# A two-layer hybrid trunk on eight cores: the mixer runs its 31-tap convolution path first, x of two token groups of the next tile is staged in idle buffers, and the last step of v's norm may run on VectorE or GpSimd

## The reference

```python
x = x + 0.5 * rms_norm(swiglu(rms_norm(x, f1_pre), f1_wg, f1_wu, f1_wd), f1_post)     # 1024 -> 2816 -> 1024
z = rms_norm(x, m_pre) @ w_in                                                        # 1024 -> 2304
a_val, a_c, a_b, b_u, b_v, c_val, c_gate = split(z)      # 3 x 256, 2 x 512, 2 x 256 columns
y_a = a_b * conv3(a_c * a_val)
v   = layer_norm(gelu(b_v), per head of 128)
y_b = gelu(b_u) * (tril(W_s) @ v + bias)                 # mixes the tokens of a chunk of 128
y_c = silu(layer_norm(conv31(c_val * sigmoid(c_gate)) + c_cb))
x = x + rms_norm(concat(y_a, y_b, y_c) @ w_out, m_post)
x = x + 0.5 * rms_norm(swiglu(rms_norm(x, f2_pre), f2_wg, f2_wu, f2_wd), f2_post)
x = x + rms_norm(sigmoid(rms_norm(x, e_pre) @ e_wg) * (p[i] @ e_wp), e_post)
```

## Time and profile before

| | us |
|---|---|
| three runs | 2700.43, 3136.25, 2699.31 |
| median | 2700.43 |
| profiled execution | 2699.21 |
| its span, slowest core (core 5) | 2697.6 |
| spans of all cores | 2689.7 to 2697.6 |
| PE busy | 2581.1 (96%) |
| DVE busy | 1148.4 (43%) |
| ACT busy | 1070.5 (40%) |
| POOL busy | 558.5 (21%) |
| mean granted PE clock by core | 0.986 to 0.989 |

### The profile page before, as it was taken

The page is one execution under the profiler, slowest core; times in us unless marked ns, Lnnn a source line. Parts: engine busy times, 40 slices in busy tenths (PEclk is TensorE's granted clock), DMA queues, the critical chain, the costliest instruction groups (busy, mean ns, idle before and its releaser), DMA issues.

```text
span 2697.6 us, 52916 instructions; the slowest of 8 cores (2689.7 to 2697.6 us)
## 1 busy us (share of the span) xinstructions
PE 2581.1 (96%) x18576; PEld 1685.2 (62%) x18576; DVE 1148.4 (43%) x2748; ACT 1070.5 (40%) x2199; POOL 558.5 (21%) x880
## 2 busy tenths in 40 slices
PE   6999989999999998999969999999999999999996
PEld 3676556666567655666637665667665676656764
DVE  2222774216621476421642137632175215672227
ACT  3123474126512356312632135731264124671235
POOL 0052212004205211200410412210052132120014
PEclk9999999999999999999989999999999999999998
DMA  8354323334344532333564454233343444423341
GB/s 161 61 89 82 69 50 64 74 65 82 64 76 79 89 65 49 63 71 65 115 159 81 74 90 65 40 75 69 65 71 75 75 71 91 64 49 71 67 82 64
DMA packets 53442, 204.38 MB, mean 76 GB/s; under 512 B 10528, under 2 KB 22592, under 8 KB 38304
## 3 DMA queue, kind: packets, MB, share of 16 engines
q0 software_dynamic: 32608, 178.81, 37.7%
q1 hardware_dynamic: 20576, 22.18, 2.8%
HBM read 371.12 MB, written 9.63 MB: 141 GB/s over the span
## 4 chain that ended last, share of the span: by engine, by line
PE 91%; ACT 3%; issue 2%; DVE 2%; DMA 1%; POOL 1%; SPq 0%; DVEq 0%; ACTq 0%; POOLq 0%
PE PS L614 89%; PE PS L620 2%; ACT L490 1%; ACT SCR L645 1%; DVE XT L656 1%; DMA XT<-xT 1%; DMA RING<-W 0%; DMA yT<-SCR 0%; SPq L684 0%; ACT SQS L645 0%; ACT R L645 0%; DVE SCR L663 0%; POOL R L651 0%; ACT PS L645 0%; POOL XT L656 0%
## 5 line engine op out<-in xcount | busy, mean ns | idle before, releaser
L614 PE MATMUL PS<-R,RING 128*128 128x256 bf16 (+2 forms) x10560 | 1617.3, 311 | 36.0 <-ACT SCR L645 19.5
L614 PEld LDWEIGHTS PS<-R,RING 128*128 128x128 bf16 x10560 | 1032.8, 98 | 541.1 <-issue 62.1
L614 PE MATMUL PS<-HIDR,RING 128*128 128x256 bf16 (+2 forms) x4992 | 767.7, 311 | 2.7 <-ACT HIDR L645 1.1
L645 ACT ACTIVATE SCR<-PS 128x256 f32<-128x256 f32 (+3 forms) x818 | 374.8, 463 | 980.0 <-PE PS L614 947.7
L656 DVE TENSOR_TENSOR HIDR<-SCR,PS 128x512 bf16<-128x512 f32 (+2 forms) x552 | 282.1, 512 | 891.6 <-PE PS L614 881.1
L614 PEld LDWEIGHTS PS<-HIDR,RING 128*128 128x128 bf16 x4992 | 489.6, 98 | 259.0 <-issue 8.0
L684 POOL DMA_DIRECT2D RING<-W x192 | 106.3, 554 | 1615.3 <-PE PS L614 1583.9
L645 ACT ACTIVATE SQS<-PS 128x256 bf16<-128x256 f32 (+2 forms) x288 | 132.0, 458 | 428.3 <-PE PS L614 426.7
L656 POOL TENSOR_TENSOR XT<-XT,SCR 128x256 f32<-128x256 f32 (+2 forms) x210 | 194.2, 934 | 397.3 <-DVE SCR L663 358.1
L663 DVE SCALAR_TENSOR_TENSOR R<-XT,VECT,PS 128x256 bf16<-128x256 f32 (+2 forms) x376 | 188.9, 565 | 70.2 <-ACT PS L645 58.7
L490 ACT ACT_TABLE_LOAD x147 | 188.6, 1283 | 2.6
(11 more groups left out here) (91 smaller groups left out, 1034.3 us busy)
## 6 DMA issues: line engine op xcount, KB each, us to landing
RING<-W POOLq DMA_DIRECT2D x116, 1024.0 KB, 8.5
RING<-W POOLq DMA_DIRECT2D x64, 704.0 KB, 6.1
RING<-W POOLq DMA_DIRECT2D x8, 768.0 KB, 6.3
XT<-xT SPq DMA_DIRECT2D x8, 512.0 KB, 9.5
XT<-xT SPq DMA_DIRECT2D x16, 256.0 KB, 9.6
yT<-SCR SPq DMA_DIRECT2D x16, 256.0 KB, 3.2
yT<-SCR SPq DMA_DIRECT2D x32, 128.0 KB, 2.1
RING<-W POOLq DMA_DIRECT2D x4, 512.0 KB, 5.0
```

The costliest lines, as they stand in the source:

```text
L614: S.add("pe", lambda e: e.matmul(out.build(), lhsT.build(), rhs.build(), start=start, stop=stop), r=[lhsT, rhs], w=[out], dur=max(n, 64) / ...
L645: return e.activation(out=out.build(), in_=in_.build(), func=func, **k2)
```

## The change

It has three parts.

1. In the mixer, `inC` becomes the first slot. Its matmuls, the convolution and the layer norm of group C are recorded with the slot numbers of the first slot. The token mix of group B goes behind `inU`. The block of code for path C is moved as it was, word for word, except that the token mix no longer stands inside it.
2. x of the first two groups of the second tile is staged in idle parts of `R1` and `HIDR` (16 transfers in place of 8). Only the third group waits for its place in `XT`. Both staged groups are loaded into `XT` later, when ACT has done a Silu of slot 9 of the tile's first feed-forward block. Slots 4 to 10 of the tile now wait for all four transfers of the third group.
3. The last step of v's norm may run on POOL as well; the layout chooses for each one.

```diff
-            plan += [(("inA", 0), 3072), (("inA", 1), 3072), (("inV", 0), 4096), (("inU", 0), 4096),
-                     (("inC", 0), 4096), (("out", 0), 4096), (("out", 1), 4096)]
+            plan += [(("inC", 0), 4096), (("inA", 0), 3072), (("inA", 1), 3072), (("inV", 0), 4096), (("inU", 0), 4096),
+                     (("out", 0), 4096), (("out", 1), 4096)]
...
-    def TS(out, in0, s1, s2, op0, op1, n, prio, eng="dve", acq=(), tag="", after=()):
+    def TS(out, in0, s1, s2, op0, op1, n, prio, eng="dve", acq=(), tag="", after=(), alt=False):
...
+              alt=("pool", 0.2 + n * 0.0021) if alt else None)
...
-            w0 = subs[0][1]
-            stage = []
-            for c0, n, _, _, _ in TILES[ti - 1]:
-                a = 8 * c0 + 4 * n
...
+            prev = TILES[ti - 1]
+            idle = []
+            for c0, n, _, _, _ in prev:
+                idle.append([R1t, 8 * c0 + 4 * n, 8 * c0 + 8 * n, 1])
+                idle.append([HIDt, JC * c0 + 16 * n, JC * (c0 + n), 2])
+            for si in range(2):
+                w0, t0_ = subs[si][1], subs[si][2]
+                chunks = []
...
+                stage[si] = chunks
+                for k in range(KC):
+                    dst = fx(chunks[k])
+                    DMA("sp", dst, raw(xv[:, k, tok0 + t0_:tok0 + t0_ + w0]), [], [dst], "c_x", 128 * w0 * 4, (0, g0 - 20 + 10 * si), tag="xs", slack=10.0)
...
+        def reload(gate):
+            if ti:
+                for si in stage:
+                    xload(si, gate, (1, g0 + 6), 0.0)
+
+        for si in range(nsub):
+            if si not in stage:
+                xload(si, [xl[0][-1]] if ti == 0 and si else [], (0, g0 + 0.01 * si - 1), 4.0 if ti else 0.0)
...
-            for i in range(slot_n[0] + 3, slot_n[0] + 11):
-                gates[i] = xl[1][:2]
+            for i in range(slot_n[0] + 4, slot_n[0] + 11):
+                gates[i] = xl[2]
...
-                src = (lambda k, si=si: fx(stage[k])) if stage and si == 0 else (lambda k, si=si: Xs(si, k))
+                src = (lambda k, si=si: fx(stage[si][k])) if si in stage else (lambda k, si=si: Xs(si, k))
...
+            if l == 0 and f == 1:
+                reload([early[0]])
...
+            wC = wload(l, ("inC", 0))
             wA = [wload(l, ("inA", 0)), wload(l, ("inA", 1))]
-            wV, wU, wC = wload(l, ("inV", 0)), wload(l, ("inU", 0)), wload(l, ("inC", 0))
+            wV, wU = wload(l, ("inV", 0)), wload(l, ("inU", 0))
...
-                               ALU.subtract, ALU.mult, 128, (0, g))
+                               ALU.subtract, ALU.mult, 128, (0, g), alt=True)
...
-                gsp = wC.g + skew(si) + 0.3
+                gsp = wU.g + skew(si) + 0.3
```

135 lines of the change are left out of this document (67 added, 68 removed).

## The result

The changed kernel takes 2667.44 us, the median of its four runs, against 2700.43 shown before. The ratio is **0.9876**, 95% interval 0.9848 to 0.9905: 1.2% faster, within the 2% of no change. Executions in which one die ran at a lower clock throughout are left out of every comparison from here on, and a time is the median of the others. The profiled execution took 2664.45 us with a span of 2662.7; before it was 2699.21 and 2697.6. The forecast was 2664, with a range of 2642 to 2694.

A forecast was written before the change was run, and what follows sets the result against it. PE was taken to bound the kernel, busy 2581.1 of 2697.6 us. Terms -20.9 (change of tile), -19.7 (mixer ends) and +4 (mixer fronts) sum to -36.6 us: 2662.6 profiled, 2664 us as median; range 2642 to 2694.

The forecast's parts named there:

- v's last step: Mixer: moving 52 of 128 norm steps from DVE to POOL costs PE nothing, bounds -4 and +4 us.
- the 5.2 us belong to the embedding step, which stays: Ahead of the change of tile, 1315 to 1355: 5.2 us belong to the embedding step and remain.
- the reading of the old wait as one for x: Change of tile: PE's 12.77 us wait was for a square whose x came late behind two weight transfers.
- The change of tile: Staging at the tile change: 23.9 us of idle and clock loss go, 3 us stay, sum -20.9 us.
- the third group's 2: New tile: 2 us of waits expected at the third group's mean matmuls, bounds 0 and 12.8.
- the first product's 1: New tile's start: the 3.18 us wait for the first product and what precedes it, 6.8 us, goes; 1 us left.
- stand earlier in ACT's list: Change of tile: staged groups' Ln and Exp come earlier on ACT, helping remove the 6.8 us around the first product.
- the third group takes over: Change of tile: third group's x goes out late, PE stops 12.8 us at its mean matmuls; 2676 us, chance 0.14.
- The mixers: Mixer ends lose 39.7 us and keep 20, so -19.7 us; mixer fronts cost +4 us, bounds 0 and 74.
- The mixer only moves its waits: Mixer ends: token mix, boundary and clock cost 36 us in place of 20; 2680 us, chance 0.15.
- The slower rival: Mixer fronts: 24 convolutions each wait 3.1 us for ACT and DVE, 74 us in all; 2733 us, chance 0.04.
- the rival: Mixer fronts and ends: shared port holds up DVE's adds, 14 us, all on the path; 2678 us, chance 0.03.

The follow-up runs named there:

- e8: Kernel before, with weight slots 3 to 10 of the second tile waiting for all four transfers of the second group's x instead of two; 2695.8 us.
- e11: Changed kernel without the gates on weight slots 4 to 10 of the second tile; 2663.5 us.
- e6: Changed kernel with every engine's order kept, but the 56 v's norm steps on POOL moved back to DVE; 2666.9 us.
- e7: Changed kernel without part three, its own orders kept, but the same 56 v's norm steps moved from DVE to POOL; 2679.8 us.
- e2: Kernel before with part one alone (convolution path first, token mix behind inU); 2698.6 us.
- e5: Kernel before with parts one and three, without the staging; 2686.7 us.
- e3: Kernel before with part three alone (v's last norm step may go to POOL); 2702.3 us.
- e4: Changed kernel without part three, v's last norm step all on DVE; 2681.3 us.
- e1: Kernel before with part two alone (staging of x and its gates); 2678.6 us.
- e13: Kernel before with parts two and three, the mixer's slots in the old order; 2683.7 us.
- e9: e4 with only the planner's duration of v's last step on DVE altered, 0.20 us in place of 0.293; 2672.1 us.
- e14: e1 with the planner's duration of v's last step on DVE at 0.20 us in place of 0.293; 2684.7 us.
- e10: e4 with the planner's duration of v's last step on DVE at 0.40 us; 2691.8 us.
- e15: e1 with the planner's duration of v's last step on DVE at 0.40 us; 2678.7 us.
- e16: e4 with the planner's duration of v's last step on DVE at 0.10 us; 2680.4 us.
- e17: e11 run again, beside the changed kernel on the same chip; 2663.2 us.
- e12: Changed kernel with the mixer's slots in the order C, V, U, A, so path A comes last; 2687.3 us.

## Why the prediction was right in its sum and wrong in its terms

Three of its steps failed: "v's last step: nothing", which was worth 13 to 15 us through the planner; "the 5.2 us belong to the embedding step, which stays", which grew by some 6 us; and the reading of the old wait as one for x. The sum hides this.

**The change of tile**: forecast -20.9, measured -18.2, and between -18.1 and -19.8 in every layout that had the staging. The weights of slot 4 on do go out behind the third group's last x, nothing waits for that x, and the 16 small loads cost nothing, as forecast. The term that fell short is "the 5.2 us belong to the embedding step, which stays". They did not stay. On the profiled core the step idles 8.8 us and loses 0.07 x 39 = 2.7 us more to the clock. Of the 3 us kept for the new tile, the third group's 2 became 0.1 and the first product's 1 became 2.1. Together that is -23.9 + 0.1 + 2.1 + 3.6 + 2.7 = -15.4, where the stretch of the two profiled cores went from 310.6 to 293.3, by 17.3; about 2 us are not placed. The staged groups' Ln and Exp stand in ACT's list at that place now, with 10 table loads in the 50 us where there were 8. The prediction named that move as a gain ("stand earlier in ACT's list") and did not price what it was moved past. That these table loads make the waits is argued from the order alone; no run takes one of them away.

The prediction also read the old wait wrongly. It said that PE waited 12.77 us for "a square whose x had not landed". The x had landed 4.0 us after its issue; ACT waited for a store of y to leave an `SCR` buffer, and the square stood behind that (e8 above). The other half of its reading, that the two weight transfers made the wait, is shown by e8, where the wait moves with them. That the term came out near its size all the same is in part luck: what had to go was a transfer of weights beside the stores of y and the loads of x, and the same edit did that. The rival "the third group takes over" was a real danger: it is what e8 does, with 9.2 us. With the staging no weight transfer stands beside the third group's four loads, with the gate (weights at 1384.80, x landed at 1384.2) or without it (e11), and 30 us of other matmuls come before the first of their mean matmuls.

**The mixers**: forecast -19.7 at the ends and +4 at the fronts, together -15.7; measured -16.0 by the stretches. Within it, idle time at the ends fell to 10.9 us, where 16 were forecast; the idle time of the mixers elsewhere rose by (23.7 - 10.9) - (30.5 - 26.2) = 8.5, where 4 were forecast; the clock gave 9.9 - 1.7 = 8.2, where 9.5 were forecast. Signs: line 620 waits no more than 0.64 us, 163 table loads, no stretch of a mixer end below 1.00, and at the change of tile about 2 us idle behind 1350 and no wait over 4: as forecast. The waits for `HIDR` at the ends are 0.5 us and not 3 to 5; what is left is the boundary's.

**v's last step**: forecast 0, within 4 us either way. That is the step that failed. As load it holds (e6, e7: the same time within 1.5 us with the steps on either engine). Its price on POOL was 832 ns and not 619, without effect. But the edit was one of the planner's inputs, and by the layout it decided 13 to 15 us, nearly all that the mixers gained. The prediction's mixer term came out right because its rows were taken from the order of the whole changed program, part three's layout included. It was the forecast of one layout, and it was told as a property of running the convolution first. Had the two parts been priced each by itself, -15.7 for the one (measured 0) and 0 for the other (measured +4 alone) would both have been wrong.

**Is convolution first better?** By the mean of five layouts against four, by 2.9 us, with a spread of 25 among the five and 2 us between sets of the same kernel: not shown. Six pairs of runs here differ in part one alone (e2 and before, e5 and e3, e4 and e1, changed and e13, e9 and e14, e10 and e15). The new order is faster by 4.8 us in their mean, with single pairs from 16.9 us faster to 13.1 us slower: not shown either. It takes the long chain off the end, which the old order could not avoid in any of its layouts (its mixers are 30 to 32 us idle in all of them). In return it makes the mixer depend on how well ACT and DVE are interleaved at the front, where it can be better (23 us idle) or worse (34).

**Rivals.** "The mixer only moves its waits" is what part one does in e2, e4 and e10, and what it did not do in the layout that was drawn. (Its 36 us are half of the old end, 19.9, and the 16 us of waits; with the 4 us of clock it would be 40 us and 2684.) The slower rival's mechanism, 1.7 us at each of 24 convolutions, is not seen in any run: on no core of any trace is a wait of line 620 of 1.7 us or more put down to DVE or ACT. The longer ones, e10's among them, are all "issue". The Trainium skill, page "SBUF — State Buffer", section "SBUF: two separate sides", says that a DVE operation with two SBUF inputs and a GpSimd operation that reads SBUF take the shared port in turn. The trace agrees for the additions: over the eight cores of the changed kernel, the 40 additions of 512 columns with no GpSimd operation beside them took 684 ns and the 296 beside one took 1158. But that one was never a moved step: not one of the 336 additions runs beside such a step. So the rival fell not because its rule is wrong here but because the two do not meet, and the additions' mean stayed (1107 ns before, 1102 after, 1086 in e3). The moved step itself is slower on GpSimd (832 ns) than the nearest row said, and what stayed on DVE went from 344 to 380 ns. Each of those runs beside a moved step, but 36 ns are little for a wait through a step of 832; no run here tests the cause.

**What stays open.** Which feature of the lists makes a layout good. Nearness of PE's order is not it (e16). Why the granted clock falls in some mixers: e2 and e9 are both near 28 us idle there and lose 8.8 and 4.3 us to it. And what the stops named "issue" are; one of them stands where the changed kernel is about 2 us slower than e17.

## What to carry to other kernels

Where a planner sets the order, an edit has two effects: what it does, and which layout is drawn. Run it with the orders held fixed, or over several meaningless changes of a planner number, before its gain is put down to it; here the meaningless numbers moved the time by up to 25 us, while a real effect (staging) stood at 18 to 20 in every layout that had it. When a square waits, look at what its engine did just before it: the list is in order, and the operation ahead may be the one that waits. And price a step that moves by what it lands in front of on its new place in the list.

## What the runs showed of the hardware that was not expected

- The clock is a cost of its own size: over the four mixers it took from 0.4 us (e11) to 13.3 us (e10), while idle time went from 22.7 (e11) to 33.6 (e10) and 38.0 (e12, 11.1 of clock). Two layouts with like idle time can differ by 5 us in it (e2, e9).
- A load of x (256 KB) landed 3.0 to 7.1 us after its issue when it went out ahead of the weights (the second group's last load, eight cores, before and e8), and 16.6 to 21.5 us after it when it went out just behind two weight transfers of 1024 KB (the eighth load, eight cores, e8). A store of y (128 KB) took 3.1 us in the median of four ahead of them and 19.3 us behind the first of them (before).
- DVE's addition of 128x512 float32 with both inputs in SBUF took 684 ns with no GpSimd operation beside it and 1158 ns in the mean with one (changed kernel, eight cores); before it was 684 and 1156.
- One `tensor_scalar` form of 128x128 from float32 to bf16 with two per-partition scalars took 344 ns on DVE when alone and 380 when a part of the steps ran on GpSimd, where each took 832 to 875; GpSimd's `DIAGA` scaling of the same shape took 619.
